# Where the condition chunks stand at the layer boundary of a two-layer trunk: one before and one behind the last turn of the hidden rows, one behind the last turned block of the sum, gathered in another PSUM bank

## What is computed

```python
def trunk_layer(x, cond, lw, lam_init, ctx=None):
    mod = (jax.nn.silu(cond) @ lw['w_ada'] + lw['b_ada'])[:, None, :]
    sh1, sc1, gt1, sh2, sc2, gt2 = jnp.split(mod, 6, axis=-1)
    h = rmsnorm(x, lw['g_norm1']) * (1.0 + sc1) + sh1
    ...                                  # three branches over h @ w_in
    x = x + gt1 * (merged @ lw['w_out'])
    h2 = rmsnorm(x, lw['g_norm2']) * (1.0 + sc2) + sh2
    x = x + gt2 * expert_choice_ffn(h2, lw['w_router'], lw['w_e_gate'], lw['w_e_up'], lw['w_e_down'])
    return x, new_ctx
```

## Time and profile before

| | |
|---|---|
| median of 3 runs | 3077.04 us (3076.04 to 3077.58) |
| the profiled execution's own time | 3078.97 us |
| its span in the trace | 3077.1 us |
| PE busy | 3011.0 us (98%) |
| DVE, ACT, POOL busy | 1239.2, 603.7, 234.4 us |
| moved by DMA | 695.55 MB, 225 GB/s over the span |

### The profile page before, as it was taken

The page is one execution under the profiler, slowest core; times in us unless marked ns, Lnnn a source line. Parts: engine busy times, 40 slices in busy tenths (PEclk is TensorE's granted clock), DMA queues, the critical chain, the costliest instruction groups (busy, mean ns, idle before and its releaser), DMA issues.

```text
span 3077.1 us, 49446 instructions
## 1 busy us (share of the span) xinstructions
PE 3011.0 (98%) x21834; PEld 1601.7 (52%) x21834; DVE 1239.2 (40%) x2404; ACT 603.7 (20%) x1349; POOL 234.4 (8%) x374
## 2 busy tenths in 40 slices
PE   7999999999999999999999999999999989999998
PEld 3555565656555444444455546666565454444443
DVE  4459553365354121221254694532644342112113
ACT  3241001144423000000032400011534230000001
POOL 0011000021001000000100100000110010000000
PEclk9999999999999999999999999999999989999999
DMA  6235432432343999999941552434224349999996
GB/s 269 97 130 191 155 146 97 140 123 74 133 157 125 408 398 397 403 399 396 373 176 55 187 199 93 151 118 144 93 74 145 142 174 410 395 405 400 395 403 269
DMA packets 102294, 695.55 MB, mean 226 GB/s; under 512 B 11786, under 2 KB 25142, under 8 KB 66752
## 3 DMA queue, kind: packets, MB, share of 16 engines
q1 hardware_dynamic: 75296, 613.97, 50.6%
q0 software_dynamic: 20736, 62.80, 7.0%
q10 hardware_dynamic: 6048, 15.62, 1.4%
HBM read 618.66 MB, written 73.68 MB: 225 GB/s over the span
## 4 chain that ended last, share of the span: by engine, by line
PE 95%; ACT 3%; DMA 1%; DVE 1%; issue 1%; DVEq 0%; POOLq 0%
PE unit L1523 14%; PE unit L997 14%; PE unit L951 12%; PE work L1526 11%; PE work L1523 7%; PE unit L1009 4%; PE unit L988 4%; PE unit L1028 4%; PE unit L1381 4%; PE unit L941 3%; PE work L965 1%; PE work L1171 1%; PE work L1194 1%; PE unit L1025 1%; DMA ring<-in_w_ada 1%; PE work L1488 1%
## 5 line engine op out<-in xcount | busy, mean ns | idle before, releaser
L997 PE MATMUL unit<-hT,ring 128*128 128x512 f32 x1024 | 452.6, 594 | 0.0
L997 PEld LDWEIGHTS unit<-hT,ring 128*128 128x128 f32 x1024 | 189.4, 190 | 217.7 <-issue 217.7
L2548 DVE SCALAR_TENSOR_TENSOR arena<-work,arena 32x256 f32<-32x256 f32 x128 | 61.7, 482 | 533.5 <-PE work L1526 532.1
L1523 PE MATMUL unit<-ring,arena 128*32 128x512 f32 x2112 | 243.4, 602 | 3.3 <-DVE arena L2536 3.3
L951 PE MATMUL unit<-hT,ring 128*128 128x512 f32 x512 | 222.2, 593 | 0.0
L1526 PE MATMUL work<-ring,arena 128*32 128x256 f32 x3072 | 183.8, 380 | 2.4 <-DVE arena L2536 2.4
L2018 ACT ACTIVATE arena<-work 128x512 f32<-128x512 f32 x32 | 19.1, 597 | 822.4 <-PE work L1541 822.4
L1629 ACT ACTIVATE xT<-unit 128x512 f32<-128x512 f32 x92 | 54.8, 596 | 590.7 <-PE unit L997 384.8
L951 PE MATMUL unit<-arena,ring 128*128 128x512 f32 x384 | 167.9, 593 | 1.6 <-ACT arena L1629 0.9
L951 PEld LDWEIGHTS unit<-hT,ring 128*128 128x128 f32 x512 | 96.2, 190 | 115.7 <-issue 115.5
L1523 PEld LDWEIGHTS unit<-ring,arena 128*32 128x32 f32 x2112 | 69.9, 111 | 149.1 <-issue 143.3
(11 more groups left out here) (447 smaller groups left out, 4201.0 us busy)
## 6 DMA issues: line engine op xcount, KB each, us to landing
ring<-in_w_e_up SPq DMA_DIRECT2D x64, 2048.0 KB, 18.5
ring<-in_w_in SPq DMA_DIRECT2D x32, 2048.0 KB, 11.6
arena<-in_w_e_gate SPq DMA_DIRECT2D x32, 2048.0 KB, 17.0
arena<-in_w_e_down SPq DMA_DIRECT2D x32, 2048.0 KB, 19.6
xT<-in_w_e_gate SPq DMA_DIRECT2D x30, 2048.0 KB, 17.1
ring<-in_w_e_down SPq DMA_DIRECT2D x30, 2048.0 KB, 17.5
ring<-in_w_ada SPq DMA_DIRECT2D x24, 2048.0 KB, 9.5
spill<-xT SPq DMA_DIRECT2D x94, 256.0 KB, 9.9
```

The lines of the kernel that those rows point to most:

```text
L997: last = mm(bank[:, :], w[:, k, m * P:(m + 1) * P], hT[:, k, 0:TS], start=k == 0, stop=k == KD - 1)
L1523: last = mm(big[SLOTP * c:SLOTP * c + SLOTP, :], x[:, s0:s0 + SLOTP], w[:, kk, 512 * (c // 2):512 * (c // 2) + 512], start=k == 0, stop=k ...
L2548: STT(y[SLS:SLS + SLOTP, 256 * c:256 * c + 256], W[5][r, 0:256], gpro[r, e:e + 1], gatep[r, :], ALU.mult, ALU.mult)
```

## The change

Chunk 0 of the next layer's condition is multiplied ahead of the last `turn_hidden`, chunk 1 right behind it and so ahead of d0 and d1 of expert 15, chunk 2 behind block 3 of the sum and chunk 3 behind block 7, ahead of `norm_sum`. The bank in which the four add up is `ps[0]` in place of `W[1]`, and chunk 0 waits for `hid_gated` of expert 15 for it. SP no longer waits for `scattered` ahead of chunk 1. ACT copies the bank out behind its eight squares and no longer between square 5 and square 6. Layer 0's condition chunks, which have no layer before them, stay as they are.

```diff
--- before.py
+++ after.py
@@ -588,8 +588,6 @@
                     name, i = PLAN[q]
                     c = chunk_no(l, name, i)
                     if name == "ada":
-                        if l and i == 1:
-                            sp.wait_ge(sig["scattered"], 16 * SUMS * l)
                         load(c, A["w_ada"][l, i])
                     elif name == "wo":
                         load(c, A["w_out"][l].rearrange("(k p) n -> p k n", p=P)[:, :, 512 * i:512 * i + 512])
@@ -956,7 +954,7 @@
 
             def ada(l, a):
                 w = chunk_in(chunk_no(l, "ada", a))
-                j, big = a % 4, W[1 if l and a < 4 else 5]
+                j, big = a % 4, ps[0] if l and a < 4 else W[5]
                 if a >= 4 and j == 0:
                     pe.wait_ge(sig["mod_ready"], 6 * l + a // 2)
                 for r in range(2):
@@ -1552,8 +1550,13 @@
                 for e in range(NE + 1):
                     if e and e < NE:
                         expert_chunk(e, "g0")
+                    if e == NE and l + 1 < DEPTH:
+                        pe.wait_ge(sig["hid_gated"], NE * (l + 1))
+                        modulate(l + 1, 0)
                     if e:
                         turn_hidden(e - 1)
+                    if e == NE and l + 1 < DEPTH:
+                        modulate(l + 1, 1)
                     if e and e < NE:
                         expert_chunk(e, "g1")
                     if e:
@@ -1568,7 +1571,6 @@
                 final = Y[(NE - 1) % NROWS][0:SL, :]
                 if l + 1 == DEPTH:
                     break
-                modulate(l + 1, 0)
                 pe.wait_ge(sig["left_copied"], NE * (l + 1))
                 pe.wait_ge(sig["right_copied"], NE * (l + 1))
                 pe.wait_ge(sig["scattered"], 16 * SUMS * (l + 1))
@@ -1586,8 +1588,9 @@
                         last = mm(W[2 + 2 * (k % 2)][:, tile_t(t)], ysum[t][:, tile_t(k)], ident,
                                   start=False, stop=t == NTS - 1)
                     last.then_inc(sig["sum_turned"], 1)
-                    if k in (1, 3, 5):
-                        modulate(l + 1, (k + 1) // 2)
+                    if k == 3:
+                        modulate(l + 1, 2)
+                modulate(l + 1, 3)
                 norm_sum(2 * l + 2)
                 for _ in fold(l + 1, 3):
                     pass
@@ -1631,7 +1634,7 @@
             def ada(l, a):
                 act.wait_ge(sig["ada_computed"], ada_no(l, a) + 1)
                 if a % 4 == 3:
-                    a_(adarow[a >= 4], W[1 if l and a < 4 else 5][:, :], ACT.Copy).then_inc(sig["mod_ready"], 1)
+                    a_(adarow[a >= 4], (ps[0] if l and a < 4 else W[5])[:, :], ACT.Copy).then_inc(sig["mod_ready"], 1)
 
             def fold(l, a):
                 act.wait_ge(sig["ada_computed"], ada_no(l, a) + 2)
@@ -1654,8 +1657,7 @@
                 for k in range(KD):
                     act.wait_ge(sig["x_added"], XADDS * l - KD + k + 1)
                     square(2 * l, k)
-                    if k == 5:
-                        ada(l, 3)
+                ada(l, 3)
                 root(l)
                 fold(l, 3)
```

## The result

| | median us | runs | lowest to highest |
|---|---|---|---|
| before | 3077.33 | 5 | 3076.04 to 3081.33 |
| after | 3094.12 | 5 | 3091.64 to 3097.62 |

The ratio is 1.0054 with a 95% interval of 1.004 to 1.0068: 16.8 us (12 to 21) slower. The forecast was 3091 with a range of 3082.5 to 3095.

The account below looks back on a forecast made before the run. PE, busy 98% of the span, was taken to bound the kernel. A sum start 16.1 us later, -3.7 of savings and +1.7 of clock gave +14.1 us: 3091 on the median of 3077.04, range 3082.5 to 3095.

Parts of the forecast that it names:

- Chunk 0: Ahead of the last turn: its load lands at 1518.9, 20.2 us after issue, so PE waits 4.7 us.
- Chunk 1: Ahead of d0: lands at 1525.0, 6.1 us (4.9 x 1.25) after chunk 0, a wait of 3.4 us.
- `ysum`: At the start of the sum: loads in at 1545.5, a wait of 6.4 us, sum 16.1 us later than before.
- four parts of five: DMA engines: share taken for the weights while both the weights' and POOL's queue have work.
- one part of three: Rival share for POOL's queue: ysum in by 1539.9, hardly waited for; +8.9 us, 3085.9; chance 0.27 together with equal parts.
- Savings: From the sum's blocks to norm_sum: 2.03 us saved twice, 0.33 given back, together -3.73 us.
- Clock: PE's granted clock falls in the new waits; only a slow stretch behind the third, for ysum, counts: +1.7 us.
- upper bound of 3.4: PE's clock loss in us if chunk 1's wait is the last and a second slow stretch counts.
- equal parts: Rival: queues share DMA engines equally, ysum in time, chunk 1 at 1528.7; +11.4 us, 3088.4; chance 0.27 with one part of three.
- the faster case: Rival: chunks 0 and 1 have landed when PE comes; -2.2 us, 3074.9; chance 0.04.
- the landings alone: Rival: only the landings of chunks 0 and 1 cost, ysum isn't late; 3081.7 to 3083.4; chance 0.15.
- the rival "worse": ysum's smaller share makes both it and the weights late, and the clock counts twice; +17 us, 3094; chance 0.09.

Follow-up runs that it names:

- e_chunk0: Kernel before with only condition chunk 0 moved ahead of the last turn of hid, in ps[0]; 3086.74 us, ratio 1.0025.
- e_hold2: Changed kernel, but w_ada chunks 2 and 3 and the first w_in chunk wait for scattered, chunk 1 does not; 3084.52 us, ratio 1.0022.
- e_pieces: Kernel before without SP's wait for scattered, condition chunks 1 and 2 each loaded in four pieces; 3084.5 us, ratio 1.0023.
- e_swap: Changed kernel with chunk 0's load issued ahead of the last expert chunk, chunk 1 behind d1, SP's wait ahead of chunk 2; 3077.85 us, ratio 0.9993.
- e_hold1: Changed kernel with SP's wait for scattered put back ahead of chunk 1, nothing else; 3095.67 us, ratio 1.0049.
- e_no_hold: Kernel before with SP's wait for scattered taken away and nothing else; 3090.65 us, ratio 1.0043.
- e_tail: Kernel before with chunk 3 behind block 7, ACT's copy behind its squares, gathered in ps[0]; 3076.15 us, ratio 0.9995.
- e_ready: Changed kernel's PE order, chunks 0 and 1 read from already landed expert slots, SP's wait back ahead of chunk 1; 3075.36 us, ratio 0.9986.
- e_warm: Changed kernel with 10 unread matmuls added between d1 and the wait for scattered; 3091.72 us, ratio 1.0041.
- e_tail_warm: e_tail with 2 unread matmuls more behind the fold, in PE's wait ahead of the first projection; 3074.29 us, ratio 0.9987.
- e_swap_warm: e_swap with 3 unread matmuls between chunk 1 and the wait for ysum, and 2 behind the fold; 3077.11 us, ratio 0.9996.

## Why the prediction was right

**Bound.** PE bounds the kernel and the loss passes one to one: 16.83 us in the distance and nothing outside it in the traces. That the medians give 16.8 as well is in part luck, since the two differ by some us in other kernels of the table.

**Chunk 0.** Forecast: a wait of 4.7 us, landing at 1518.9. Measured: 5.48 and 1521.4, of which 1.9 is this trace's late start; e_chunk0 shows it alone. The Trainium skill's fixed cost plus bytes (DMA: Bandwidth & Descriptors, "Anatomy of one DMA"), which the page gives for the path of POOL's transfers and not of SP's, would have had it there long before; the rows of before and after say 20.2 and 20.8 us. What stands behind this is an uneven backlog: in the trace of before eight of the load's 16 increments come from 1507.6 to 1509.5, the other eight from 1517.3 to 1518.9. Why half of the engines are 9 us behind is open.

**Chunk 1.** Forecast at 1525.0, measured at 1527.1, 1525.2 on the clock of the trace of before. The 5.7 us between the landings of chunks 0 and 1 stand against the 4.9 x 1.25 = 6.1 of the sum.

**`ysum`.** Forecast to hold up the sum until 1545.5; it started at 1548.75, or 1546.9 less the 1.88. That its time is set by the weight chunks beside it is shown by e_hold2 (9.4 us to landing with one of them in place of 26.89 with four), and the four parts of five at an engine where both queues have work by the order of the packets (79%, under e_pieces). Averaged over all 16 engines the share was near the rival's one part of three (from 1522 to 1532 in the changed kernel 65.8% to 34.9%), by which `ysum` would have been in at 1539.9 and hardly waited for. It came 7 us after that, since the average hides the half of the engines that still had weights: chunk 1's increments come eight from 1518.2 to 1519.1 and eight from 1524.6 to 1527.1. The sum went by the engines that are furthest behind, and the increments bear that out.

**Savings.** Forecast -3.73 us. From the start of block 0 to `norm_sum` it was 21.63 us (1533.23 to 1554.86) and is 17.89 (1555.75 to 1573.64): -3.74.

**Clock.** This is the term that was mis-sized most: +1.7 forecast, 3.2 measured in the prompt part, near the upper bound of 3.4 but for another reason, since that bound counted a second slow stretch. The price came from a stretch behind a 2.1 us wait, where the clock was low for part of five us. Behind 9.4 us of waiting it was low from the first instruction on for some seven. The slow stretch behind the first wait (3.48 us for chunk 0) was swallowed by the wait for chunk 1, and behind the second there was none (1.90 us for chunk 1).

**Sum.** 17.5 (late start of the sum) - 3.7 + 3.2 = 17.0 against 16.1 - 3.7 + 1.7 = 14.1; the first projection's start gives 16.8. The missing 2.7 us are about 1.4 of `ysum` and 1.5 of the clock. The rivals fell: equal parts and one part of three by the wait of 9.40 us for `ysum`, which they had at none or next to none, the faster case by the wait of 5.48 us for chunk 0, and the landings alone by the last `ysum` load, 26.89 us in place of 7.6. The measured time is at the upper end of the range and the same as that of the rival "worse" (+17, 3094), but not by its account: chunk 1 wasn't later than forecast, and the clock didn't count in two stretches; one cost twice its price.

## What to carry to other kernels

Work that is moved up to fill an engine's short wait must be checked against the landing of what it reads, not against the moment its load is issued or the bytes over the bandwidth: here 2 MB took 20 us, because half of the engines were behind. A wait that holds back a prefetch can be what protects a small, urgent transfer on another queue; compare the packets of both, since on an engine with work from both the queue with the larger ones gets the larger part (79% with 16 KB against 4 KB). A share averaged over all engines hides this. A wait of PE can cost more than its length, because the clock can fall in it (3.2 us more behind the wait of 9.4); matmuls that nobody reads kept the clock up there.

## What the runs showed that was not expected

Whether the clock falls behind the 2.1 us wait ahead of the first projection differs from execution to execution of the same code there: its 64 passes took 9.04 us before, 9.05 after, 9.01 in e_hold2 and e_swap, 8.88 in e_hold1, 8.83 in e_chunk0, but 7.80 or 7.81 in e_no_hold, e_tail, e_ready, e_pieces and e_warm, all behind a wait of 2.1 us. With matmuls in the wait (e_tail_warm, e_swap_warm) it was 7.80 both times, which five of the eleven others reach without them, so two traces can't show that the matmuls did it. The landing of chunk 0's load varied too, 18.9 to 21.6 us in the eleven kernels that issue it at the same place, and with it PE's wait for it, 3.59 to 5.48 us in the five that use it ahead of the turn.
